# Decay scores of a gated linear attention, level by level: six levels as 32x32 blocks in four column groups, two as rectangles

## The reference

```python
q = silu(q_raw); f = lb + (1 - lb) * sigmoid(f_raw); k = 1 - f
# per head, with b = cumsum(log f) along the tokens
diff  = b[t] - b[s]                         # per key channel
decay = exp(where(s <= t, diff, -inf))
attn[t, s] = sum_k q[t, k] * k[s, k] * decay[t, s, k]
o = (q * exp(b)) @ S + attn @ v
S = exp(b_last) * S + (k * exp(b_last - b)).T @ v
```

## Time and profile before

| | |
|---|---|
| median of 3 runs | 4106.85 us (4068.61 to 4108.99) |
| profiled execution | 4125.37 us |
| its span | 4123.6 us, mean granted TensorE clock 0.939 |
| PE busy | 3762.0 us (91%) |
| DVE, ACT, POOL busy | 2281.5, 1321.4, 268.2 us |
| this stage | from about 2616 to 3519 us of the span |

### The profile page before, as it was taken

How to read it: one execution, slowest core, us unless ns; L and a number is a source line. 1 busy time by engine, 2 the same in 40 slices (tenths; PEclk the granted TensorE clock), 3 DMA queues, 4 the chain that set the end, 5 groups by cost and what they waited for, 6 DMA issues and landing times. The chain is left out here.

```text
span 4123.6 us, 55232 instructions
## 1 busy us (share of the span) xinstructions
PE 3762.0 (91%) x22472; PEld 2394.1 (58%) x22472; DVE 2281.5 (55%) x3988; ACT 1321.4 (32%) x2225; POOL 268.2 (7%) x233
## 2 busy tenths in 40 slices
PE   7789998988989979898898988899999999899998
PEld 4477645774654457744765654477667676344443
DVE  3475357745663456356765654266666667533453
ACT  3342244424543234144423446211111111131003
POOL 0110000000000011010000000121111222000000
PEclk9898798978999989899998999999999999999999
DMA  4223212102033332311112022211111110312331
GB/s 159 92 80 96 68 40 74 52 24 95 13 106 106 111 104 79 103 31 58 52 59 97 13 93 75 67 36 36 38 39 41 36 36 11 127 56 62 94 116 51
DMA packets 300860, 281.17 MB, mean 68 GB/s; under 512 B 16945, under 2 KB 273073, under 8 KB 300609
## 3 DMA queue, kind: packets, MB, share of 16 engines
q1 hardware_dynamic: 300608, 277.65, 20.8%
HBM read 204.27 MB, written 73.33 MB: 67 GB/s over the span
## 5 line engine op out<-in xcount | busy, mean ns | idle before, releaser
L3291 DVE SCALAR_TENSOR_TENSOR cv<-glu,params,cv 128x1024 f32<-128x1024 f32 x240 | 338.5, 1410 | 6.1
L1451 PE MATMUL ps<-hT,w_cols 128*128 128x512 f32 x576 | 255.6, 603 | 13.6 <-PEq L158 13.6
L399 PE MATMUL ps<-hT,w_cols 128*128 128x512 f32 x448 | 204.0, 616 | 3.2 <-PEq L158 3.2
L1451 PEld LDWEIGHTS ps<-hT,w_cols 128*128 128x128 f32 x576 | 111.2, 194 | 153.0 <-issue 151.0
L3589 PE MATMUL ps<-hT,wr 128*128 128x512 f32 x360 | 161.7, 592 | 0.0
L399 PEld LDWEIGHTS ps<-hT,w_cols 128*128 128x128 f32 x448 | 87.8, 198 | 116.5 <-issue 116.5
L3113 PE MATMUL ps<-w_i,hT 128*128 128x128 f32 x1152 | 132.6, 275 | 0.0
L3113 PEld LDWEIGHTS ps<-w_i,hT 128*128 128x128 f32 x1152 | 130.6, 192 | 0.0
L3267 POOL TENSOR_TENSOR Sp<-Sp,Rp 128x520 f32<-128x520 f32 (+1 forms) x56 | 88.4, 1579 | 639.4 <-DVE W L3308 639.4
L3097 PE MATMUL ps<-hT,w_f 128*128 128x347 f32 x384 | 116.0, 462 | 6.9 <-DMA w_f<-in_w_in 6.9
L3104 PE MATMUL ps<-hT,w_q 128*128 128x512 f32 x256 | 111.9, 595 | 9.2 <-DVE attn L3316 9.2
(11 more groups left out here) (909 smaller groups left out, 7709.3 us busy)
## 6 DMA issues: line engine op xcount, KB each, us to landing
w_cols<-in_w_in SPq DMA_DIRECT2D x32, 512.0 KB, 3.9
wr<-in_w_in SPq DMA_DIRECT2D x24, 512.0 KB, 5.1
hT_hbm<-hT SPq DMA_DIRECT2D x2, 4096.0 KB, 14.6
hT<-hT_hbm SPq DMA_DIRECT2D x2, 4096.0 KB, 13.6
fh<-hT_hbm SPq DMA_DIRECT2D x16, 512.0 KB, 4.6
fh_again<-hT_hbm SPq DMA_DIRECT2D x16, 512.0 KB, 4.6
x<-in_x SPq DMA_DIRECT2D x8, 512.0 KB, 8.3
ahead<-kb_hbm SPq DMA_DIRECT2D x16, 256.0 KB, 3.4
```

The source lines that it names most:

```text
L399: q = pe.matmul(ps[:, proj_bank(n, b), :], lhsT=wc[:, n % 3, k, :], rhs=hT[:, k, P + b * 512:P + (b + 1) * 512], start=(k == 0), stop=(k = ...
L1451: q = pe.matmul(ps[:, proj_bank(n, b), :], lhsT=wc[:, n % 3, k, :], rhs=hT[:, k, P + b * 512:P + (b + 1) * 512], start=(k == 0), stop=(k = ...
L3291: vec.scalar_tensor_tensor(out=cv[:, h % 2, :], in0=src, scalar=w, in1=cv[:, h % 2, :], op0=ALU.mult, op1=ALU.add).then_inc(*VEC(f"tap{h}_ ...
```

## The change

It touches only the head loop of the second block.

- Levels n = 0 to 5 (n <= OWN = NLEV - 2 = 5): their wanted entries lie in the four 32x32 blocks on the diagonal of a tile. `pairs` computes just those, for each tile four matmuls of contraction 128 with 32 weight columns and 32 moving columns, block j to PSUM partitions 32j to 32j+31. All of a level now lies in 256 columns of one bank, bank 3 for even n and 4 for odd n (`scores(n)`). `kept` copies under the mask into a new tensor attn_own (one copy of 128x256).
- Level n = 6: two matmuls a tile, of blocks (0, 1) and (2, 3), to partitions 0 to 31 and 64 to 95. Level n = 7: one a tile, 64 weight columns and 64 moving columns, to partitions 0 to 63. Both are wholly wanted and need no mask.
- ACT puts attn together: `spread` (four copies of 32x256 from attn_own to the diagonal blocks, after the last masked copy), `beside` (level 6, two copies from PSUM), `top` (level 7, one copy from PSUM). The entries below stay zero, as cleared at the start.
- Waits: pairs n waits for kept n - 2 in place of kept n - 1; q's first half waits for `beside`, its second half for `top`; outputs wait for `top`; kept 0 of the next head waits for `spread` in place of the outputs.
- kept 6 and kept 7 leave DVE's order. The masks come in by eight small transfers in place of one.

```diff
-            at = sbuf(st, "attn", [P, SEQ])
+            at = sbuf(st, "attn", [P, NT, P])
+            at_own = sbuf(st, "attn_own", [P, NT, 32])
-            up = sbuf(st, "up", [P, NLEV, P])
+            up = sbuf(st, "up", [P, NLEV, 32])
+            OWN = NLEV - 2
+            def block_of(j):
+                return slice(32 * j, 32 * j + 32)
+            def scores(n):
+                return ps[:, BANK_Y + n % 2, 0:32 * NT].rearrange("p (t n) -> p t n", n=32)
...
-                    sp.dma_start(up[:, :, :].rearrange("p k n -> p (k n)"), io["consts"][:, C_N - NLEV * P:C_N]).then_inc(*DMA("up"))
+                    for j in range(4):
+                        own = io["consts"][block_of(j), C_N - NLEV * P:C_N].rearrange("p (k n) -> p k n", n=P)
+                        sp.dma_start(up[block_of(j), 0:OWN, :], own[:, 0:OWN, block_of(j)]).then_inc(*DMA("up"))
+                        at_i = C_AT["ident"][0] + 32 * j
+                        sp.dma_start(up[block_of(j), OWN, :], io["consts"][block_of(j), at_i:at_i + 32]).then_inc(*DMA("up"))
...
-                            pe.wait_ge(*VEC[f"kept{h}_{n - 1}"])
                             pe.wait_ge(*VEC[f"W{h}_{n - 1}"])
-                        for t in range(NT):
-                            u = slice(t * P, (t + 1) * P)
-                            a, b = (k_[:, P + t * P:P + (t + 1) * P], q_[:, u]) if n == 0 else (W[:, (n - 1) % NWB, u],) * 2
-                            q = pe.matmul(tile_of(BANK_Y, t), lhsT=a, rhs=b, start=True, stop=True)
+                        if n >= 2:
+                            pe.wait_ge(*VEC[f"kept{h}_{n - 2}"])
+                        if n == NLEV:
+                            for t in range(NT):
+                                u = W[:, (n - 1) % NWB, t * P:(t + 1) * P]
+                                q = pe.matmul(ps[0:64, BANK_Y + n % 2, t * 64:(t + 1) * 64], lhsT=u[:, 0:64], rhs=u[:, 64:P], start=True, stop=True)
+                        else:
+                            for t in range(NT):
+                                a, b = (k_[:, P + t * P:P + (t + 1) * P], q_[:, t * P:(t + 1) * P]) if n == 0 else (W[:, (n - 1) % NWB, t * P:(t + 1) * P],) * 2
+                                for j in range(4) if n <= OWN else (0, 2):
+                                    q = pe.matmul(ps[block_of(j), BANK_Y + n % 2, t * 32:(t + 1) * 32], lhsT=a[:, block_of(j)],
+                                                  rhs=b[:, block_of(j if n <= OWN else j + 1)], start=True, stop=True)
...
-                            pe.wait_ge(*VEC[f"kept{h - 1}_{NLEV}"])
+                            pe.wait_ge(*ACT[f"beside{h - 1}"])
                         project_half("q", h, BANK_Y, 0)
+                        if h > 0:
+                            pe.wait_ge(*ACT[f"top{h - 1}"])
                         project_half("q", h, BANK_Y, 1)
...
+                    def spread(h):
+                        act.wait_ge(*VEC[f"kept{h}_{OWN}"])
+                        for j in range(4):
+                            q = act.copy(at[block_of(j), :, block_of(j)], at_own[block_of(j), :, :])
+                        q.then_inc(*ACT(f"spread{h}"))
+                    def beside(h):
+                        act.wait_ge(*PE[f"pairs{h}_{OWN + 1}"])
+                        for j in (0, 2):
+                            q = act.copy(at[block_of(j), :, block_of(j + 1)], scores(OWN + 1)[block_of(j)])
+                        q.then_inc(*ACT(f"beside{h}"))
+                    def top(h):
+                        act.wait_ge(*PE[f"pairs{h}_{NLEV}"])
+                        act.copy(at[0:64, :, 64:P], ps[0:64, BANK_Y + NLEV % 2, :].rearrange("p (t n) -> p t n", n=64)).then_inc(*ACT(f"top{h}"))
...
                         if h > 0:
+                            top(h - 1)
                             keys(h - 1)
...
                         act.activation(sgg[:, :], two(BANK_Z), FN.Silu).then_inc(*ACT(f"g{h}"))
+                        spread(h)
+                        beside(h)
+                    top(KD - 1)
                     keys(KD - 1)
...
-                            vec.wait_ge(*PE[f"o{h - 1}"])
-                        mask = ident if n == 0 else up[:, n - 1, :]
-                        for b in range(2):
-                            q = vec.copy_predicated(at[:, b * 512:(b + 1) * 512].rearrange("p (t n) -> p t n", n=P), rep(mask, 4).bitcast(U32),
-                                                    ps[:, BANK_Y + b, :].rearrange("p (t n) -> p t n", n=P))
+                            vec.wait_ge(*ACT[f"spread{h - 1}"])
+                        if n > 0:
+                            vec.wait_ge(*VEC[f"kept{h}_{n - 1}"])
+                        q = vec.copy_predicated(at_own[:, :, :], rep(up[:, n - 1 if n else OWN, :], NT).bitcast(U32), scores(n))
...
-                            kept(h - 1, NLEV)
                             taps(h - 1, 6)
                             states(h - 1)
...
-                        kept(h, 6)
                         taps(h, 4)
-                    kept(KD - 1, NLEV)
                     states(KD - 1)
```

More of the change, by code:

```diff
@@ L3145, in outputs @@
                     def outputs(h):
-                        pe.wait_ge(*VEC[f"kept{h}_{NLEV}"])
+                        pe.wait_ge(*ACT[f"top{h}"])
                         pe.wait_ge(*VEC[f"qR{h}"])
@@ L3150, in outputs @@
                             u = slice(t * P, (t + 1) * P)
-                            pe.matmul(tile_of(BANK_Z, t), lhsT=v[:, P + t * P:P + (t + 1) * P], rhs=at[:, u], start=True, stop=False)
+                            pe.matmul(tile_of(BANK_Z, t), lhsT=v[:, P + t * P:P + (t + 1) * P], rhs=at[:, t, :], start=True, stop=False)
                             q = pe.matmul(tile_of(BANK_Z, t), lhsT=Sst[:, t, :], rhs=qR[:, u], start=False, stop=True)
@@ L3352, in _ @@
                     vec.tensor_tensor(e2[:, 1, :], l[:, :, 1], mxl[:, :], ALU.subtract).then_inc(*VEC("lb_shift"))
-                    vec.memset(at[:, :], 0.0)
+                    vec.memset(at[:, :, :], 0.0)
+                    vec.memset(at_own[:, :, :], 0.0)
                     vec.memset(Rp[:, 0:P], 1.0)
```

## The result

The changed kernel takes 4051.3 us (median of 4 runs, 4025.6 to 4054.3), the kernel before in the same runs 4107.9 us. The ratio is 0.9865, 95% interval 0.982 to 0.991: faster by about 1.4%. The forecast was 4057 us. Later rounds gave 0.985 (0.980 to 0.990; e9).

What follows compares the result with a forecast made beforehand. PE was taken to bound the head loop; gains of 28.2, 10.1, 9.2 and 2.3 us less 0.4 sum to 49.4, giving 4057 us from 4106.85. Its own range was 4033 to 4066 us, the whole 4022 to 4099.

Steps and rivals of the forecast that it cites:

- levels 0 to 5: Head loop on PE: as 32x32 blocks at 15.1 ns a pass, a level costs 1.20 us against 1.79; 28.2 us gained.
- levels 6 and 7: Head loop on PE: fewer or narrower passes save 0.86 and 0.59 us, over seven heads 10.1 us gained.
- the stall before q: PE's wait before the q projection for DVE's last masked copy goes, seven times 1.3 us: 9.2 us gained.
- last head: End of the head loop: state sums start 7.3 us after level 6 in place of 9.6; 2.3 us gained.
- first head: Without squares between glu_a and level 1, the values wait for glu a little: 0.4 us lost.
- PE as the bound: Head loop: PE, busy 106.7 of 108.0 us, sets the pace; taking work off DVE alone would gain nothing.
- the issue pace that the 14.1 shows: First block's 32x32x32 matmuls at 14.1 ns each, read as an issue pace; 15.1 ns a pass was taken, above it.
- Change of shape: Switching between undivided and small matmuls on PE costs 0.10 us in and about 0.17 out; 0.23 us a level taken.
- Rival A: Levels on PE: column groups overlap less than fourfold at 128 rows, about 28 ns a pass, 4099 us; chance 0.26 with its like.
- Rival B: Levels on PE: column groups do not overlap at all, 56.4 ns a pass, 4192 us; chance 0.05.
- Rival C: PE's instruction supply falls behind the added passes, 1.5 us or more in each of 48 bursts, 4130 us; chance 0.08.
- Rival D: Head loop: another engine takes over as bound, DVE needing over 103 us a head; called hardly likely, others together 0.03.

Runs made afterwards that it cites:

- e9: The changed kernel again, without an edit, as a reference on the same chip: median 4036.2 us, ratio to the kernel before 0.985; one head 100.91 us.
- e5: The changed kernel with levels 0 to 5 contracted over 32 of the 128 channels, operands contiguous: one head 100.87 us against 100.91.
- e6: The changed kernel with levels 0 to 5 contracted over 32 channels and the moving operand at a stride of 32 elements: one head 102.89 us against 100.91.
- e3: The changed kernel with the moving operand of levels 0 to 6 given twice side by side, 64 columns in place of 32: one head 103.33 us against 100.91.
- e2: The changed kernel with each matmul of levels 0 to 5 issued twice, 128 passes a level in place of 64: one head 104.11 us against 100.91.
- e4: The changed kernel with the moving operand of levels 0 to 5 at a stride of 32 elements, all 128 rows: one head 105.4 us against 100.91.
- e1: The changed kernel with the loops swapped, all tiles of one column group before the next group, same 64 passes: one head 108.20 us against 100.91.
- e12: The kernel before, undivided 128x128 levels, with their moving operand at a stride of 8 elements: one head 124.18 us against 109.39.
- e11: The changed kernel with the moving operand of levels 0 to 5 at a stride of 2 elements: one head 100.93 us against 100.91.

## Why the prediction was right, point by point

The sum was 49.4 us and the stage gained 64.6. All in all the mechanism was as told, and one term was much too small. That the forecast of 4057 us lies so near the measured 4051.3 is partly luck: the two medians differ by 56.6 us, 8 less than the stage gained, and what lies ahead of the stage varies by more than that from run to run.

| term | predicted, us | measured, us |
|---|---|---|
| levels 0 to 5 | 28.2 | 48 x 0.90 = 43 |
| levels 6 and 7 | 10.1 | 7 x 1.54 = 10.8 |
| the stall before q | 9.2 | 7 x 1.56 = 10.9 |
| last head | 2.3 | 1.5 |
| first head | -0.4 | -1.0 |
| sum | 49.4 | 65.2 (stage: 64.6) |

- **PE as the bound:** right, before and after.
- **First head:** 0.6 us for glu and 0.4 for the Sigmoid of glu_b, two of the waits shown above; only the first was named.
- **Levels 0 to 5, the mis-sized term.** The step that failed is "it is the row with all 128 rows and is above the issue pace that the 14.1 shows". There is no issue pace of 14.1 ns: e5 and e6 show that it comes from the stride of that operand. With nothing to hold it at 14, a pass goes to 9.0 ns, inside the bounds of 7 and 56.4 but near the lower, and a level costs 0.69 + 0.10 + 0.10 = 0.89 us in place of 1.20. The row that was taken for a floor kept the sum from it. It also hid a slip in the scaling: 30.3 ns was a pass of 64 moving columns. Halved for four groups in place of two it is 15.1, and that is the price of 64 columns, which e3 measured at 14.3. Halved again for 32 columns the same row gives 7.6, near what came.
- **Change of shape:** 0.23 us expected. In the changed kernel the four passes of squares start at 2972.03 and would end at 2973.74, the level starts at 2973.84: 0.10 in. Its 64 passes at 9.0 ns would end at 2974.42, the values start at 2974.53: 0.11 out. So far the 0.23 is right. But the values then take 5.56 us from their start to the next level's, where it was 5.36, and only 0.10 of that is the next level's way in: 0.10 more is lost behind the change, which the forecast did not count. Together it is 0.31 a level, 0.08 more than in the sum. Of the 15 us by which this term was too small, the price of a pass makes 48 x 64 x 6.1 ns = 19, and this takes 4 back.
- **Level 6 and 7:** a pass of level 6 costs (0.70 - 0.20)/31 = 16 ns (22 taken), one of level 7 (1.15 - 0.22)/15 = 62 ns (60.6 taken). Together they fill what is left of 3024.94 - 3008.00 once f's 48 passes (14.02) and the key turn's 8 (0.89) are off, 2.03 us against 3.57: 1.54 gained, 1.45 expected.
- **The stall:** it went, and nothing took its place. It was worth 1.56 us and not 1.30, because the profile counts idle time from the modelled end of the matmuls. From start to start the key turn's 8 passes end at 3065.60 and q starts at 3067.05, and q's first pass then is 0.1 us longer, its weight load starting with it, where in the changed kernel it starts 0.11 us ahead (3024.83 against 3024.94).
- **DVE:** the copies fell from 10.73 to 2.64 us a head, as worked out. But DVE as a whole fell only from 72.7 to 67.5 and not by the 8.1 that were forecast: the 30 taps of a head rose from 42.8 to 45.7 us. Three taps with POOL's products beside them, before and then after (timelines of DVE and POOL):

```profile
3025.69 1.08 POOL L3270 TENSOR_TENSOR Rp<-Rp 128x512 f32<-128x512 f32 x1
3025.91 4.58 DVE L3291 SCALAR_TENSOR_TENSOR cv<-glu,params,cv 128x1024 f32<-128x1024 f32 x3
```

```profile
2987.64 5.38 DVE L3332 SCALAR_TENSOR_TENSOR cv<-glu,params,cv 128x1024 f32<-128x1024 f32 x3
2988.68 1.94 POOL L3311 TENSOR_TENSOR Rp<-Rp 128x512 f32<-128x512 f32 x1
```

  In the second both engines are slower at once. Running beside taps is not enough to tell them apart, since both products do: before, it began 0.22 us ahead of the taps and took 1.08 us, after, it began 1.04 us into them and took 1.94. The shorter masked copies moved the taps ahead against POOL's work; that this is the cause is argued and not tested. DVE isn't the bound, so it costs nothing.

- **ACT:** 18.05 to 20.85 us, 2.8 in place of 3.0; a 32x256 copy took 0.40 us, as estimated.
- **Last head:** the state sums start 8.05 us after level 6 (3419.85 against 3411.80), 7.3 were expected, 9.6 it was:

```profile
3411.80 0.70 PE L3146 MATMUL ps<-W 128*32 128x32 f32 x32
...
3415.72 1.00 ACT L3244 COPY kS<-ps 128x1024 f32<-128x1024 f32 x1
3416.87 2.94 PE L3161 MATMUL ps<-v,kS 128*128 128x128 f32 x16 [2.28 <-ACT kS L3244]
3419.85 0.29 DVE L3374 COPY Sst<-ps 128x128 f32<-128x128 f32 x1 [4.52 <-PE ps L3161]
```

  ACT's chain was forecast well (key_values starts 5.07 us after level 6, 5.3 expected). What was missed: key_values takes 2.94 us in place of 1.95. The granted clock from 3416.80 to 3419.90 us is 0.66, so for most of it the lower level, 1.2 GHz; in the 5 us before, in which PE stood for 2.28 us, it is 1.00. That is a matter of the single run. With the same wait of 2.28 us, key_values takes 2.02 us at clock 1.00 in e2 and e6, 2.60 in e5, 2.96 in e9 and 3.55 in e4:

```profile
3431.82 2.02 PE L3161 MATMUL ps<-v,kS 128*128 128x128 f32 x16 [2.28 <-ACT kS L3244]
```

  In that run (e2) the sums start 7.14 us after level 6, as good as the 7.3 of the forecast. So the path was right, and the 0.9 us over it are the clock's.
- **Rival A** (less overlap at 128 rows) did not come: 9.0 ns. The floor of about 25 ns from start to start (the Trainium skill, "TensorE: Matmul & The Clock Gate", the section on the clock gate) does not hold for passes dealt over column groups. Within one group the 27.2 ns of e1 agree with it and with streaming alike. The rule of the same page's packing part, that weight loads overlap matmuls only of other row groups, is not borne out: here all share their rows, a weight load lasts 0.11 us, and passes start 9.0 ns apart.
- **Rival B** did not come. Even one group after the other a pass costs 27.2 ns (e1), so the upper bound of 56.4, made from the strided row, was twice too high.
- **Rival C** did not come, but e2, with twice the passes in a level, shows its first signs, so the margin was about a factor of two, as the 6.8 us against 3.45 said.
- **Rival D:** no.

## What to carry to other kernels

Where only blocks on the diagonal of a score tile are wanted, compute only those, dealt over the column groups in turn: the order of the loop alone was worth 27.2 against 9.0 ns a pass. When a neighbouring row serves as a price, compare its access patterns as well as its shape. Put small matmuls side by side, since each stretch of them costs about 0.3 us around it, and look at the moving operand's stride.

## What the runs showed of the hardware that I had not expected

- Strided moving operands in fp32: 1.81 ns a column in place of 0.87 at a step of 8 elements in an undivided pass (e12), 1.78 at a step of 32 with 32 rows a group (e6), 2.55 with four groups on the same 128 rows (e4), and no price at a step of 2 (e11).
- Four column groups share all 128 rows without loss at 64 moving columns (14.3 ns a pass, 57 ns a round, e3) and come to 9.0 ns at 32.
- Rows are free: 8.8 ns with 32 rows, 9.0 with 128 (e5).
- Taps on DVE took 1.43 us on average in a head before and 1.52 after, beside POOL products that lengthened as well (22.8 to 24.6 us a head), with not an edit to either.
- A change between 128x128 and 128x32 passes costs about 0.10 us in, 0.11 out and 0.10 in the passes that follow.
